# A depthwise convolution as 128x32 column tiles with four taps stacked in the contraction, its norm and projection moved ahead, and VectorE's mixers in fewer operations

## The reference

```python
z = hn @ w_in[l]                       # 256 x 2564: all inputs of the four branches
# a: differential attention, 4 heads, two score maps (q1 k1, q2 k2), a = p1 - lam * p2
# b: gated causal depthwise convolution
a, g = jnp.split(z_b, 2, axis=-1)      # 256 channels each
y = a * jax.nn.sigmoid(g)
y = conv(y, w, width 31, causal, one filter per channel) + b
o_b = jax.nn.silu(_layer_norm(y, ng, nb_))
# c: gelu and a 128 x 128 spatial gate; d: attention with forget gates ("fox"), 4 heads
mixed = jnp.concatenate([o_a, o_b, o_c, o_d], axis=-1)
h = h + g2[:, None, :] * (mixed @ w_out[l])
```

## Time and profile before

| | us |
|---|---|
| median of 3 runs | 2318.02 (2317.71 to 2319.38) |
| the profiled execution | 2322.53 |
| its span | 2320.7 |
| PE busy | 2254.3 (97%) |
| DVE busy | 1615.1 (70%) |
| ACT busy | 1095.3 (47%) |
| POOL busy | 97.2 (4%) |

### The profile page before, as it was taken

How to read it: one execution, slowest core, us unless ns; L and a number is a source line. 1 busy time by engine, 2 the same in 40 slices (tenths; PEclk the granted TensorE clock), 3 DMA queues, 4 the chain that set the end, 5 groups by cost and what they waited for, 6 DMA issues and landing times.

```text
span 2320.7 us, 31791 instructions
## 1 busy us (share of the span) xinstructions
PE 2254.3 (97%) x11791; PEld 1900.5 (82%) x11801; DVE 1615.1 (70%) x1847; ACT 1095.3 (47%) x1286; POOL 97.2 (4%) x145
## 2 busy tenths in 40 slices
PE   7999999999999999999999999999999999999998
PEld 6887877887788797788788889988878888998887
DVE  6886886886777687666655678675566557867555
ACT  3434544434443454534444465654444446565433
POOL 1000031000000103000000000000000000000000
PEclk9999999999999998999999999999999999999999
DMA  9986534886587463466555554356556655434653
GB/s 303 338 306 195 190 119 136 298 308 227 195 296 268 147 208 110 160 219 221 180 192 185 181 164 128 110 196 202 193 169 199 194 185 157 134 110 164 212 186 109
DMA packets 323522, 452.24 MB, mean 195 GB/s; under 512 B 31590, under 2 KB 269032, under 8 KB 323432
## 3 DMA queue, kind: packets, MB, share of 16 engines
q1 hardware_dynamic: 320456, 440.98, 57.6%
q0 software_dynamic: 2704, 8.99, 1.2%
q10 hardware_dynamic: 272, 1.05, 0.1%
HBM read 449.92 MB, written 1.05 MB: 194 GB/s over the span
## 4 chain that ended last, share of the span: by engine, by line
PE 90%; DVE 5%; ACT 3%; issue 1%; POOL 1%; DMA 0%; SPq 0%; DVEq 0%; ACTq 0%
PE ps L598 20%; PE ps L600 20%; PE ps L599 20%; PE ps L591 5%; PE ps L592 5%; PE ps L593 5%; PE ps L1158 2%; PE ps L761 2%; PE ps L910 1%; DVE wlo L1928 1%; PE ps L743 1%; PE ps L688 1%; PE ps L746 1%; PE ps L744 1%; PE ps L1018 1%
## 5 line engine op out<-in xcount | busy, mean ns | idle before, releaser
L1928 DVE TENSOR_TENSOR wlo<-raw,whi 128x2048 fp32r<-128x2048 f32 (+1 forms) x348 | 791.9, 2278 | 358.2 <-ACT whi L1308 354.7
L1308 ACT ACTIVATE whi<-raw 128x2048 fp32r<-128x2048 f32 x346 | 660.2, 1910 | 298.5 <-PE ps L600 239.2
L598 PE MATMUL ps<-whi,xl 128*128 128x512 f32 x1472 | 591.5, 402 | 0.0
L600 PE MATMUL ps<-whi,xh 128*128 128x512 f32 x1472 | 574.2, 390 | 0.0
L599 PE MATMUL ps<-wlo,xh 128*128 128x512 f32 x1472 | 573.9, 390 | 0.0
L598 PEld LDWEIGHTS ps<-whi,xl 128*128 128x128 f32 x1472 | 276.6, 188 | 61.2 <-issue 4.3
L600 PEld LDWEIGHTS ps<-whi,xh 128*128 128x128 f32 x1472 | 276.3, 188 | 59.9
L599 PEld LDWEIGHTS ps<-wlo,xh 128*128 128x128 f32 x1472 | 276.8, 188 | 58.3 <-issue 4.3
L591 PE MATMUL ps<-xl,whi 128*128 128x256 f32 x864 | 251.1, 291 | 1.6 <-DVE wlo L1928 1.6
L598 PE MATMUL ps<-whi,hidl 128*128 128x512 f32 x640 | 252.0, 394 | 0.0
L600 PE MATMUL ps<-whi,hidh 128*128 128x512 f32 x640 | 249.2, 389 | 0.0
(11 more groups left out here) (394 smaller groups left out, 2512.3 us busy)
## 6 DMA issues: line engine op xcount, KB each, us to landing
raw<-in_ffn_w_in_dram SPq DMA_DIRECT2D x176, 512.0 KB
arena<-in_ada_w_dram SPq DMA_DIRECT2D x144, 512.0 KB, 5.9
raw<-in_w_in_dram SPq DMA_DIRECT2D x54, 1024.0 KB
raw<-in_ffn_w_out_dram SPq DMA_DIRECT2D x44, 1024.0 KB
raw<-in_w_ffn_gate_dram SPq DMA_DIRECT2D x88, 512.0 KB
raw<-in_w_ffn_up_dram SPq DMA_DIRECT2D x88, 512.0 KB
raw<-in_w_ffn_down_dram SPq DMA_DIRECT2D x44, 1024.0 KB
raw<-in_w_out_dram SPq DMA_DIRECT2D x16, 1024.0 KB
```

Of the source, the lines that this page charges most:

```text
L598: pe.matmul(o, al, wh, start=start, stop=False, **kw)
L600: return pe.matmul(o, ah, wh, start=False, stop=stop, **kw)
L1308: act.activation(whi[:, k % 3, :], raw[:, k % 3, :], ACT.Copy).then_inc(hi_done, 1)
L1928: tt(a[0], a[1], a[2].bitcast(F32), ALU.subtract).then_inc(lo_done, 1)
```

## The change

**PE.** `taps` and `rest_of_taps` are gone. `convolve` does all 31 taps in one place, behind `z(10)` and ahead of `turn(0)`. Partition 32j+c of its moving operand is channel c of a group of 32, shifted by j tokens (j = 0 to 3), so that one matmul sums four taps; its stationary operand is 128x32, and the four channel groups i go to four column tiles of PE. With eight tap groups and two channel halves it is 64 matmuls by 256 tokens a layer. The mean over channels comes right behind `attend(0)`, the squares' sum behind the fox scores, and `ORDER` projects the convolution before fox.

**POOL.** `diagonals` is gone. `tap_operands` writes the stationary operands with two 128x1024 operations early in the stage. `spread_rows` issues 16 DMAs from `ypad` to the moving operand, 32x2x284 values each (72.7 KB, 1.16 MB in all), into the tiles of `f`, `dq`, `dk`, `ca` and `cg`, which must have been read for the last time: it waits for `conv_in` and for the second scores.

**ACT.** `conv_done` moves ahead of the copy of gelu's output; the square, `rs` and the sigmoid table of the convolution's norm move ahead of `hi(k0 + 13)` and of the second `turned_out`. For event 0 the square that `newton` needs is now ACT's.

**DVE.** The late taps are gone. `newton` has one operation less. gelu has one less, the layer norm's root nine small ones where there were twelve. `logits` of this mixer are eight `tensor_tensor_reduce` where there were two `scalar_tensor_tensor` and two reductions. The difference of the two probability maps is eight operations where there were three.

**Setup.** The convolution's weights come by 16 small DMAs in place of one.

```diff
@@ numbers and orders @@
-        ORDER = (2, 0, 3, 1)
+        ORDER = (2, 0, 1, 3)
@@ setup: a stage of weights by 16 DMAs @@
-            (stage[0:124, 1, :], rows(conv_w, "l j (c p) -> (l j c) p"))]
+        for l in range(LAYERS):
+            for g in range(TAPGROUPS):
+                n, at = min(4, CONVK - 4 * g), 64 * l + 8 * g
+                stage_rows.append((stage[at:at + 8, 1, 0:32 * n].rearrange("p (j c) -> p j c", j=n),
+                                   conv_w[l, 4 * g:4 * g + n].rearrange("j (x c) -> x j c", c=32)))
@@ PE @@
+                def convolve():
+                    pe.wait_ge(taps_ready, l + 1)
+                    pe.wait_ge(s["gmixed"], l + 1)
+                    pe.wait_ge(conv_spread, 256 * (l + 1))
+                    half = TAPGROUPS // 2
                     for ch in range(2):
+                        for g in range(TAPGROUPS):
+                            w = tap_weights(m)[g // half]
+                            for i in range(4):
+                                ins = pe.matmul(ps[32 * i:32 * i + 32, PVB, ch * S:ch * S + S], w[:, g % half, ch, i, :],
+                                                spread[:, i, ch, 4 * g:4 * g + S], start=(g == 0),
+                                                stop=(g == TAPGROUPS - 1), skip_group_check=True,
+                                                tile_position=(0, 32 * i))
                     ins.then_inc(s["convsum"], 1)
...
                 diff_scores(1)
-                taps(0, 9)
                 z(9)
                 head_stat(L, 1, 1, blk64, sq8, [ps[:, 6, :], ps[:, 7, :]])
-                taps(9, 18)
                 z(10)
+                convolve()
                 turn(L, 0, S0)
-                taps(18, 24)
                 pe.wait_ge(s["foxqk"], l + 1)
                 attend(0, "dv", 7)
-                taps(24, 30)
+                cx, csq = halves("ca"), halves("cg")
+                pe.wait_ge(s["conv_done"], 2 * l + 2)
+                for ch in range(2):
+                    ins = pe.matmul(ps[:, 0, 0:S], ones_d[:, :], cx[:, ch, :], start=(ch == 0), stop=(ch == 1))
                 head_stat(L, 2, 2, blk64, u8[:, 1536:2048], [ps[:, 6, :]])
...
-                taps(30, TAPS)
-                rest_of_taps()
@@ DVE @@
                 dve.wait_ge(y_ready, e + 1)
-                st(tt(t, y, y, ALU.mult))
+                if not squared:
+                    st(tt(t, y, y, ALU.mult))
                 st(stt(t, ms, EPS, t, ALU.add, ALU.mult))
-                st(ts(t, t, -0.5, 1.5, ALU.mult, ALU.add))
-                st(tt(r, y, t, ALU.mult))
+                st(stt(r, t, -3.0, y, ALU.add, ALU.mult))
...
+                    for h in range(4):
+                        dve.tensor_tensor_reduce(tile[:, h, 0:P], sc0[:, h, :], mask[:, 0:P], scale, NEG, ALU.add, ALU.max,
+                                                 accum_out=mx[:, h:h + 1])
...
-                (a, ra), (b, rb) = scaled(S1)
-                tt(a, a, ra, ALU.mult)
-                st(tt(b, b, rb, ALU.mult))
-                tt(s0f, s0f, s1f, ALU.subtract).then_inc(s["pnorm"], 1)
+                for h in range(4):
+                    for c, keys in ((h, slice(0, P)), (4 + h, slice(P, 3 * P))):
+                        ins = stt(S0[:, h, keys], S1[:, h, keys], rsum[:, c:c + 1], S0[:, h, keys], ALU.mult, ALU.add)
+                ins.then_inc(s["pnorm"], 1)
...
-                late_taps(PETAPS, PETAPS + 5)
+                dve.wait_ge(s["cmean"], l + 1)
+                mean = ps[:, 0, 0:S].unsqueeze(1).to_broadcast([P, 2, S])
+                stt(ca2, mean, -4.0, ca2, ALU.mult, ALU.add).then_inc(s["craw"], 1)
...
-                tiles(14, 15)
+                tiles(14, 16)
@@ POOL @@
+            def spread_rows(l):
+                pool.wait_ge(s["conv_in"], l + 1)
+                until(s["scores"], l * ROUNDS[0] + 2)
+                for j in range(4):
+                    for i in range(4):
+                        pool.dma_start(spread[32 * j:32 * j + 32, i], ypad[32 * i:32 * i + 32, :, j:j + SPREAD]
+                                       ).then_inc(conv_spread, 16)
```

More of the change, by code:

```diff
@@ L316, in before0, with tap_weights @@
             return sum((k in ON_PE) == pe for k in range(i))
[L318 to L321 removed]
+        def tap_weights(m):
+            return [t.rearrange("p (g c i o) -> p g c i o", g=TAPGROUPS // 2, c=2, i=4)
+                    for t in (gate[:, m % 2, :], acc[:, 2048:3072])]
+        tap_eye = prm[:, 32:64]
+        gu_tmp = nrm[:, 0:2, :].rearrange("p a b -> p (a b)")
         def accb(n, a):
@@ L1224, in mix0 @@
                 scores(L, st, fq, lambda r, w, c: fk[r:r + w, c, :], lambda h: (64 * (h % 2), h // 2), 64, True)
-                taps(30, TAPS)
-                rest_of_taps()
+                pe.wait_ge(s["sq"], seq(L, SQS, 4))
+                for ch in range(2):
+                    ins = pe.matmul(ps[:, 0, S:2 * S], ones_d[:, :], csq[:, ch, :], start=(ch == 0), stop=(ch == 1))
+                ins.then_inc(ms_ready, 1)
                 pe.wait_ge(s["o"], seq(L, OUTS, 2))
@@ L1230, in mix0 @@
                 turn(L, 1, S1)
-                pe.wait_ge(z_copied[0], l * NZ[0] + 11)
                 modulation(m, 0)
-                cx, csq = halves("ca"), halves("cg")
-                pe.wait_ge(s["conv_done"], 2 * l + 2)
-                for ch in range(2):
-                    ins = pe.matmul(ps[:, 0, 0:S], ones_d[:, :], cx[:, ch, :], start=(ch == 0), stop=(ch == 1))
-                ins.then_inc(s["cmean"], 1)
                 attend(1, "fv", PVB)
-                pe.wait_ge(s["sq"], seq(L, SQS, 4))
-                for ch in range(2):
-                    ins = pe.matmul(ps[:, 0, S:2 * S], ones_d[:, :], csq[:, ch, :], start=(ch == 0), stop=(ch == 1))
-                ins.then_inc(ms_ready, 1)
                 project(0, 1).then_inc(unit_used, 1)
@@ L1741, in mix0 @@
                 copied(L, zi["gu"])
-                act.wait_ge(s["scores"], seq(L, ROUNDS, 2))
-                act.activation(zt["dq"], zt["gu"], ACT.Square).then_inc(s["gu_sq"], 1)
+                act.activation(gu_tmp, zt["gu"], ACT.Square, scale=GELU_A ** 0.5).then_inc(s["gu_sq"], 1)
                 turned_out(L, 0, PT1)
                 act.wait_ge(s["gu_t"], 2 * l + 2)
-                act.activation(zt["dq"], zt["dq"], ACT.Sigmoid, scale=-GELU_B).then_inc(s["gu_e"], 1)
+                act.activation(gu_tmp, gu_tmp, ACT.Sigmoid, scale=-GELU_B).then_inc(s["gu_e"], 1)
                 logs_and_exps()
+                act.wait_ge(s["convsum"], l + 1)
+                for ch in range(2):
+                    act.activation(zt["ca"][:, ch * S:ch * S + S], ps[:, PVB, ch * S:ch * S + S], ACT.Identity,
+                                   bias=prm[:, CB + 2 * l + ch:CB + 2 * l + ch + 1]).then_inc(s["conv_done"], 1)
                 act.wait_ge(s["gu"], l + 1)
@@ L2446, in gelu_in @@
                     dve.wait_ge(s["gu_sq"], 2 * l + nth)
-                    st(ts(tmp, tmp, GELU_A, 1.0, ALU.mult, ALU.add))
-                    tt(tmp, tmp, z, ALU.mult).then_inc(s["gu_t"], 1)
+                    stt(tmp, tmp, 1.0, z, ALU.add, ALU.mult).then_inc(s["gu_t"], 1)
                 def head_norm(e, y, gains, names, done):
-                    newton(st, L.event(e), stat2, y, u8h[1], u8h[0])
+                    newton(st, L.event(e), stat2, y, u8h[1] if e else sq8h[0], u8h[0], e == 0)
                     for i, name in enumerate(names):
@@ L2456, in head_norm @@
                     ins.then_inc(s[done], 1)
-                def late_taps(first, last):
-                    for tap in range(first, last):
-                        for ch in range(2):
-                            o, col = zt["dk"][:, ch * S:ch * S + S], CW + 62 * l + 2 * tap + ch
-                            w, y = prm[:, col:col + 1], ypad[:, ch, tap:tap + S]
-                            if tap == PETAPS:
-                                ins = ts(o, y, w, None, ALU.mult)
-                            else:
-                                ins = stt(o, y, w, o, ALU.mult, ALU.add)
-                        st(ins)
                 lo(L, k0 + 2)
@@ L2572, in mix0 @@
                 tt(b, b, rb, ALU.mult).then_inc(s["pnorm"], 1)
-                tiles(15, 16)
-                lo(L, k0 + 13)
-                dve.wait_ge(s["cmean"], l + 1)
-                mean = ps[:, 0, 0:S].unsqueeze(1).to_broadcast([P, 2, S])
-                stt(ca2, mean, -4.0, ca2, ALU.mult, ALU.add).then_inc(s["craw"], 1)
                 newton(st, L.event(3), ps[:, 0, S:2 * S], nrm[:, 0, :], nrm[:, 1, :], nrm[:, 2, :])
@@ L2680, in _ @@
                 if n in (1, 4):
-                    diagonals(n // 3)
+                    tap_operands(n, n // 3)
+                    spread_rows(n // 3)
                 if n == 5:
```

173 lines of the change are left out of this document (92 added, 81 removed).

## The result

| | us |
|---|---|
| median before, 4 runs | 2317.86 (2316.45 to 2319.38) |
| median after, 4 runs | 2296.28 (2294.87 to 2299.07) |
| ratio | 0.9905, 95% interval 0.9893 to 0.9917 |
| spans of the profiled executions | 2320.7 before, 2293.1 after |

A forecast was written before the change was run, and what follows sets the result against it. PE, busy 97% of the span, was taken as the bound. Taps -43.8, convolution +14.2, new waits +7.2, old wait -1.3, setup +1.3, DVE +0.2 make -22.2 us: median 2318.0 to 2295.8, forecast 2296, own range 2289 to 2300.

The forecast's parts named there:

- What goes and what comes: On PE: 51.1 us of taps, of which 43.8 go; 64 matmuls a layer come, 14.2 us for both layers.
- the half clock stays: PE's tap stretches: time lost to half clock falls on whatever stands there next, so 7.3 us of the taps' time stay.
- The step from two column tiles to four: Convolution on PE: four column tiles run at once, though the row showed two; 7.1 us a layer.
- The three new waits: PE waits for ACT's two transpose copies and `conv_done`, formerly under taps: 1.6, 0.7 and 1.25 us, 7.2 for both layers.
- The wait that should go: PE's 0.6 us wait for ACT's sum at a modulation disappears: 1.3 us for two layers.
- fox's chain: Fox's probabilities, first logits operation to last scaling: 9.6 us before, 8.8 after, with fused logits at 2.9.
- The cover: PE's work behind the fox scores, one statistic and two half units: 9.4 us, 0.6 longer than the chain it hides.
- Rival C: POOL's 16 transfers: stretched issues make PE wait at the convolution; 2306 us at 1.1 an issue, 2332 at 2.0; chance 0.05.
- break-even: POOL's transfers: at 1.6 us an issue the last lands at 334 and the gain of 11 us a layer is used up.
- projected 30 us later: Weight loads during POOL's transfers: 3.7 us of their stream is taken, but the delayed units are projected 30 us later; cost nothing.
- The term of 1.3 us: Setup: fifteen more DMAs on SP's queue ahead of the first weights cost PE 1.3 us, ends 0 and 4.
- the sum: Whole kernel: all terms added, -43.8 + 14.2 + 7.2 - 1.3 + 1.3 + 0.2 = -22.2 us.

The follow-up runs named there:

- old logits: Changed kernel with the logits in the four operations of before instead of eight fused ones: 2307.3 us, ratio 0.9937.
- one load: Changed kernel with the convolution's weights staged by one DMA as before, in place of 16: 2293.4 us, ratio 0.9897.
- tile after tile: Changed kernel with the 64 matmuls reordered, all eight tap groups of one column tile before the next tile: 2330.2 us (one run).
- 64 transfers: Changed kernel with each of POOL's 16 transfers cut into four by tokens, 64 issues a layer: 2337.5 us (one run).

## Why the prediction was right

**What bounds.** PE in full, as read from the earlier trace rows: it is busy 97% of the span before and after.

**What goes and what comes.** 51.1 of taps went, of which 1.3 were PE's two waits for a diagonal of POOL's, one a layer, as here:

```profile
337.83 1.94 PE L1158 MATMUL ps<-arena,side 128*128 128x256 f32 x6 [0.67 <-POOL side L2655]
```

That the half clock stays was right: by the table it took 22.2 us of the two mixers before and takes 23.9 now, though the taps are gone. Windows over the same stretches, before:

```profile
227.60:417.20 189.60, 177.80 (x1012) 0.94 0.45 147
786.30:980.00 193.70, 182.45 (x1041) 0.95 0.46 148
```

and after:

```profile
225.00:402.00 177.00, 163.06 (x1046) 0.93 0.51 165
771.10:952.50 181.40, 169.17 (x1075) 0.93 0.51 165
```

`convolve` took 7.05 us, said 7.1. The step from two column tiles to four held, and what it rests on is the order: the experiments with one and two tiles among neighbours price it at 15 and 4.4 us a layer. The Trainium skill's ratio of 3.07, measured with four row tiles (TensorE: Matmul & The Clock Gate, Part 3: Packing small matmuls — row/col tiling), would give an estimated 8.8 us; these four column tiles reach 27.1 / 7.05 = 3.8.

**The three new waits.** Said 1.6, 1.25 and 0.7; measured 1.63, 1.13 and 0.9. They are real time: with the transpose ahead of the convolution the first two were gone and the kernel was 4.0 us faster. The wait that should go went.

**What is hidden.** The fused logits took 2.3 us, not 2.9, the lower end, and fox's chain 8.3 (348.32 to 356.59), not 8.8. The cover was mis-sized by more than that: it was said to be 9.4 us, 0.6 longer than the chain, and `turn(1)` starts at 356.75, after 8.4, with 0.16 to spare. That this is an edge is shown by the old logits, with 1.3 and 0.7 us of wait at once. The transfers landed 7.7 and 4.2 us ahead, where 2 to 4 were said: an issue took 0.53 us, not 0.59, and the start was earlier. In other profiles that cover is smaller, down to 1.3 us (one load, first mixer). Rival C's stretched issue did not come. (Its break-even is counted with a landing of 3 us, where its other figure has 4.3; with 4.3 it is at 1.5 us an issue, not 1.6.) The growth to 3100 ns that the Trainium skill tells of (SBUF — State Buffer, SBUF: two separate sides) doesn't occur in this stretch either; but that is for a DVE copy, and DVE ran none here, so that rule itself isn't tested.

**Not foreseen.** The units that land while PE runs ahead. The prediction let the loads' delay fall on units "projected 30 us later"; but ACT does the `hi` of such a unit ahead of a copy that PE needs at once, and so its landing counts at once, long before its projection. It cost 1.4 us in the profiled execution, and up to 3.9 in others (5.7 against 1.8).

**Setup.** The term of 1.3 us was mis-sized, and its size is below what the execution scatters: the profiles of the slower start give 0.3, but start times of one and the same setup lie up to 3.6 us apart. It stays open between 0 and about 1. The profiled executions are 27.6 us apart and the medians 21.6, since the profiled one of before was 4.5 above its median and had the slow start, and that of after, 2294.9, the lowest of its four.

**Where luck helped.** Each mixer's 12.5 stands 0.6 above the 11.85 that the sum gives (22.2 and the 1.5 of setup and DVE, halved), and the table takes that roughly apart. The two mixers are 25.0 us shorter: 3.5 more of waits, 1.7 more of clock loss, so 30.2 less of everything else. The sum had, counted in the same way, 4.6 more of waits (7.2 less the 1.3 at the modulations and the 1.3 at the diagonals), nothing for the clock, and 28.3 less of the rest. So the work was under-rated by 1.9 us and the waits over-rated by 1.1, and the clock took 1.7 of that back; among the waits a late load (1.4 more) and a shorter wait at the start of the next stage (0.8 in place of 1.9 in both layers) stood against each other. The mechanism was right and its terms within some 2 us; that 2296 meets the median is luck beyond that, for the runs' interval is 5.5 us wide and the clock loss alone scatters by more than the errors.

## What to carry to other kernels

Narrow matmuls on different column tiles run side by side only if they are neighbours in the list: loop over the tiles innermost. When filler work is taken off the bound engine, list what ran under it (here two ACT copies and a load) and put other independent work of that engine there; one swap of two lines gave 4.0 and 5.4 us in two pairs of kernels, beside 21.6 for the whole change. An instruction that only waits for a load should not stand ahead of one that the bound engine needs at once: moving it was worth some 10 us where the load came late, and nothing measurable where it mostly came in time. Before a difference of a few us is put down to a wait, compare the granted clock over stretches that begin and end at the same work.

## What the runs showed of the hardware

- Passes of 256 columns with a 128x32 stationary operand: 55 ns each with four column tiles among neighbours, 90 with two, 171 with one (between changes of tile 0.21 us), at the full clock.
- At a change of column tile the next tile's first pass starts ahead of the last three of the old tile, which stand before it in the list (323.94 against 324.15, 324.37 and 324.58 us).
- POOL issues a transfer within SBUF in 0.53 us, for 18 KB and for 72 KB, beside a busy DVE; they land 2.1 us (18 KB, median of the first mixer) and 2.0 to 4.3 us (72 KB, medians 3.6 and 2.4) after issue.
- Eight fused operations (multiply, add, maximum) over 128x128 and 128x256 take 2.3 us with their accumulator reads of 0.08; the four separate ones 3.7.
- The loads between 10 and 30 us run at 330 GB/s in some executions and 362 to 382 in others, with the same instructions; PE's granted clock in them is 1.00 and 0.75 to 0.80. The units at 110 us stand up to 3.6 us apart.
- The two mixers of a profiled execution lose 15.4 to 25.6 us to half clock, 22.2 before the change, with tile after tile 29.0 and with 64 transfers 39.3; two executions of the changed kernel lose 23.9 and 25.6.
